# Latent attention scores: the pass of rotated query highs with rotated key lows as 64-row tiles in two halves of TensorE's array

## What is computed

```python
q = jnp.concatenate([q_nope, q_rope], axis=-1)      # 128 plain + 64 rotated dimensions per head
k = jnp.concatenate([k_nope, kr broadcast to all heads], axis=-1)   # the rotated key is shared by the heads
ml = softmax_attention(q, k, v)                     # scale 192 ** -0.5, 512 queries x 768 keys
```

## Time and profile before

| | |
|---|---|
| median of three runs | 2656.37 us (2654.33 to 2659.18) |
| profiled execution, its own time | 2650.61 us |
| its span, first to last instruction | 2648.8 us |
| PE busy | 2523.6 us, 95% |
| DVE / ACT / POOL busy | 60% / 44% / 29% |
| mean granted TensorE clock | 0.980 of full speed |
| share of PE in the chain that ended last | 79% |

### The profile page before, as it was taken

One profiled execution on the slowest core, in us unless ns is written; L12 is line 12 of the kernel. 1 busy time (PEld: TensorE's weight loads), 2 busy tenths in 40 slices (PEclk: granted clock), 3 DMA queues, 4 the chain that ended last, 5 costly groups with the idle time before them and its releaser, 6 DMA issues.

```text
span 2648.8 us, 41477 instructions
## 1 busy us (share of the span) xinstructions
PE 2523.6 (95%) x15654; PEld 2237.8 (84%) x15654; DVE 1587.1 (60%) x2593; ACT 1162.3 (44%) x2137; POOL 773.9 (29%) x462
## 2 busy tenths in 40 slices
PE   7999999999889899899999999999899999899999
PEld 5999999696856787899999978998778868788887
DVE  4877785978677615877866768733776661411111
ACT  4544432555578413323323346634666662322221
POOL 3000012626357332445645520000000013344443
PEclk9999999899889999999999999999999999999999
DMA  7344455021220320332444423424763302122222
GB/s 283 129 143 142 141 173 208 32 73 60 103 96 17 120 80 25 104 112 98 150 135 136 136 80 128 167 92 143 241 205 124 111 32 80 66 98 99 102 97 80
DMA packets 124354, 307.22 MB, mean 116 GB/s; under 512 B 12448, under 2 KB 38048, under 8 KB 122784
## 3 DMA queue, kind: packets, MB, share of 16 engines
q1 hardware_dynamic: 103312, 259.94, 28.9%
q10 hardware_dynamic: 20880, 45.10, 4.9%
HBM read 249.10 MB, written 55.84 MB: 115 GB/s over the span
## 4 chain that ended last, share of the span: by engine, by line
PE 79%; DVE 8%; ACT 6%; issue 5%; POOL 1%; DMA 1%; ACTq 0%; DVEq 0%; SPq 0%; POOLq 0%
PE ps L565 15%; PE ps L567 15%; PE ps L566 15%; PE ps L1603 4%; PE ps L1604 3%; PE ps L1605 3%; PE ps L1498 3%; PE ps L1474 2%; PE ps L1484 2%; PE ps L882 2%; ACT prb L2288 1%; PE ps L1378 1%; PE ps L1380 1%; PE ps L1379 1%; DVE nmd L2809 1%
## 5 line engine op out<-in xcount | busy, mean ns | idle before, releaser
L546 POOL TENSOR_TENSOR Wl<-raws,Wh 128x2048 fp32r<-128x2048 f32 (+3 forms) x82 | 320.4, 3908 | 1495.8 <-ACT Wh L540 1486.8
L565 PE MATMUL ps<-Hh,Wh 128*128 128x384 f32 (+2 forms) x1088 | 375.6, 345 | 8.5 <-DVE xT L3285 2.8
L567 PE MATMUL ps<-Hh,Wl 128*128 128x384 f32 (+2 forms) x1088 | 370.2, 340 | 0.0
L566 PE MATMUL ps<-Hl,Wh 128*128 128x384 f32 (+2 forms) x1088 | 370.1, 340 | 0.0
L540 ACT ACTIVATE Wh<-raws 128x2048 fp32r<-128x2048 f32 (+3 forms) x125 | 204.9, 1640 | 180.4 <-PE ps L567 138.7
L3274 DVE SCALAR_TENSOR_TENSOR xT<-ps,mod,xT 128x384 f32<-128x384 f32 (+3 forms) x174 | 84.5, 533 | 277.1 <-PE ps L567 276.8
L565 PEld LDWEIGHTS ps<-Hh,Wh 128*128 128x128 f32 x1088 | 205.1, 189 | 18.1 <-DVE Hl L2814 5.0
L566 PEld LDWEIGHTS ps<-Hl,Wh 128*128 128x128 f32 x1088 | 205.3, 189 | 6.2 <-issue 1.9
L567 PEld LDWEIGHTS ps<-Hh,Wl 128*128 128x128 f32 x1088 | 205.1, 189 | 4.8
L2939 DVE SCALAR_TENSOR_TENSOR ybuf<-ubuf,vec,ybuf 128x770 f32<-128x770 f32 x144 | 155.5, 1080 | 56.9 <-ACT ybuf L1806 42.4
L565 PE MATMUL ps<-H1h,Wh 128*128 128x512 f32 (+1 forms) x368 | 141.7, 385 | 4.4 <-DVE H1l L2814 3.4
(11 more groups left out here) (494 smaller groups left out, 6725.6 us busy)
## 6 DMA issues: line engine op xcount, KB each, us to landing
raws<-in_slabs SPq DMA_DIRECT2D x218, 512.0 KB, 4.5
adl<-in_ada ACTq DMA_DIRECT2D x48, 512.0 KB, 3.7
ada<-in_ada SPq DMA_DIRECT2D x32, 512.0 KB, 3.8
raws<-in_slabs SPq DMA_DIRECT2D x62, 256.0 KB, 3.4
chunks<-obuf ACTq DMA_DIRECT2D x48, 256.0 KB, 2.1
ada<-in_ada SPq DMA_DIRECT2D x8, 1024.0 KB, 4.9
chunks<-uh SPq DMA_DIRECT2D x17, 384.0 KB, 2.8
lows<-ul SPq DMA_DIRECT2D x17, 384.0 KB, 2.6
```

The source lines that it names most:

```text
L546: nc.gpsimd.tensor_tensor(Wl[n % 2][:, 0:w], raw[n % 2][:, 0:w], Wh[n % 2][:, 0:w].bitcast(f32), ALU.subtract).then_inc(sig("slab_lo"), 1)
L565: nc.tensor.matmul(o, lhs(c)[0], rhs(c, t0, t1)[0], start=(s == 0), stop=False)
L566: nc.tensor.matmul(o, lhs(c)[0], rhs(c, t0, t1)[1], start=False, stop=False)
L567: last = nc.tensor.matmul(o, lhs(c)[1], rhs(c, t0, t1)[0], start=False, stop=(s == k - 1))
```

## The change

The fifth term leaves the loop over the four ranges. Behind it stand four matmuls of 64 rows each, one for each range, in the order 1, 0, 3, 2 of `four`. Block 0 takes the rotated query's high rows from mrs, partitions 0 to 63; block 1 takes them from a new tile mrt, partitions 64 to 127, into which a seventh transfer loads them. Each multiplies by the half of krl that lies in the same partitions. The product low x low, which the fifth term held before, is no longer computed. The matmul of range 0 raises at_beside and the one of range 2 waits for it. As every item now raises at_beside once, the count shared becomes 12 * i + n. ml_in counts 112.

```diff
--- before.py
+++ after.py
@@ -467,6 +467,7 @@
         das, dak, mkh, mkl, mqh, mql, mrs = ([place(f"{n}{j}", at + (b0, b1)[j], shape, f32r) for j in range(2)] for n, at, b0, b1, shape in (
             ("das", 0, 64, 81, [2, LAT]), ("dak", 8, 64, 81, [2, T]), ("mkh", 0, 20, 95, [T]), ("mkl", 0, 0, 98, [T]),
             ("mqh", 0, 12, 101, [LAT]), ("mql", 0, 14, 103, [LAT]), ("mrs", 0, 6, 105, [LAT])))
+        mrt = [place(f"mrt{j}", kb, [LAT], f32r) for j, kb in enumerate((117, 85))]
         krh, krl = place("krh", 28, [T], f32r), place("krl", 68, [T], f32r)
         av, mv = [place("av0", 16, [T]), place("av1", 138, [T])], [place("mv0", 3, [T]), place("mv1", 78, [T])]
         uqh = [place(f"uqh{j}", 148 + 3 * j, [T], f32r) for j in range(2)]
@@ -1443,7 +1444,7 @@
             def scores(i, n):
                 kind, hh, x = ITEMS[n % 12]
                 if x == 0:
-                    name, count = (f"da_in{hh}", 64) if kind == "da" else (f"ml_in{hh}", 96)
+                    name, count = (f"da_in{hh}", 64) if kind == "da" else (f"ml_in{hh}", 112)
                     pe.wait_ge(sig(name), past(name) + count * (i + n // 12) + count)
                     if kind == "ml":
                         pe.wait_ge(sig("kr_in"), past("kr_in") + 64)
@@ -1451,9 +1452,9 @@
                 b0 = 3 * ((n + 1) % 2)
 
                 four = ((1, 0, 256, b0 + 1, 256), (0, 0, 512, b0, 0), (0, 512, T, b0 + 1, 0), (1, 256, T, b0 + 2, 0))
+                shared = 12 * i + n
                 if kind == "da":
                     tq = slice(x * P, (x + 1) * P)
-                    shared = 8 * i + sum(ITEMS[m % 12][0] == "da" for m in range(n))
                     for z, y in BESIDE:
                         b, t0, t1, bank, c = four[z]
                         if (z, y) == (2, 0):
@@ -1469,10 +1470,19 @@
                     tq = slice((2 * x + b) * P, (2 * x + b + 1) * P)
                     qh, ql, qr, kh, kl = (t[hh] for t in (mqh, mql, mrs, mkh, mkl))
                     terms = ((qh[:, tq], kh[:, t0:t1]), (qh[:, tq], kl[:, t0:t1]), (ql[:, tq], kh[:, t0:t1]),
-                             (qr[:, tq], krh[:, t0:t1]), (qr[:, tq], krl[:, t0:t1]))
+                             (qr[:, tq], krh[:, t0:t1]))
                     for y, (q, k) in enumerate(terms):
-                        ins = nc.tensor.matmul(ps[:, bank, c:c + t1 - t0], q, k, start=(y == 0 and (b, t0) != (0, 512)),
-                                               stop=(y == len(terms) - 1), skip_group_check=True)
+                        nc.tensor.matmul(ps[:, bank, c:c + t1 - t0], q, k, start=(y == 0 and (b, t0) != (0, 512)),
+                                         stop=False, skip_group_check=True)
+                for z in (1, 0, 3, 2):
+                    b, t0, t1, bank, c = four[z]
+                    rows, tq = slice(64 * b, 64 * b + 64), slice((2 * x + b) * P, (2 * x + b + 1) * P)
+                    if z == 2:
+                        pe.wait_ge(sig("at_beside"), shared + 1)
+                    ins = nc.tensor.matmul(ps[:, bank, c:c + t1 - t0], (mrs, mrt)[b][hh][rows, tq], krl[rows, t0:t1],
+                                           start=False, stop=True, skip_group_check=True)
+                    if z == 0:
+                        ins.then_inc(sig("at_beside"), 1)
                 ins.then_inc(sig("at_s"), 1)
 
             def turned(i, n, j):
@@ -3929,6 +3939,8 @@
             for half, name in enumerate(("chunks", "lows")):
                 sp.dma_start(mrs[hh][64 * half:64 * half + 64, :].bitcast(f32), scr[name][24 + i, 64 * hh:64 * hh + 64, 0:LAT])\
                     .then_inc(sig(f"ml_in{hh}"), 16)
+            sp.dma_start(mrt[hh][64:P, :].bitcast(f32), scr["chunks"][24 + i, 64 * hh:64 * hh + 64, 0:LAT])\
+                .then_inc(sig(f"ml_in{hh}"), 16)
 
         def heads_ml_queries(sp, i, hh):
```

## The result

| | before | after |
|---|---|---|
| median (22 runs each) | 2656.72 us | 2660.81 us |
| ratio after to before | | 1.0015, 95% interval 1.0009 to 1.0021 |
| span of the profiled execution | 2648.8 us | 2658.8 us |
| PE busy | 2523.6 us | 2532.2 us |

The ratio times 2656.7 is 4.0 us, with 2.4 to 5.6 as its interval. The forecast was +5.1 us, 2661.5 in a range of 2655.5 to 2665. The loss is smaller than the 0.2% that the prediction took as the least that can be told from no change, but with 22 runs on each side the interval does not hold zero: the change costs time.

A forecast was written before the change was run, and what follows sets the result against it. The prediction took PE, busy for 95% of the span, as the bound. Latent items 15 x 0.31 + 0.16 = 4.8 us plus 0.3 for the transfer made 5.1 us, carried to the median 2661.5 us, range 2655.5 to 2665.

The forecast's parts named there:

- Way in: PE going from full-width matmuls to the 64-row tiles in a latent item: the drain costs 0.093 us.
- Wait: Fourth tile's weight load waits for the signalling 256, whose signal comes in order of issue: load at T0 + 0.56 us.
- T0: Start time of the first pair of 64-row tiles in the latent item's new pass.
- Way out: PE's return from tiles to full width: work back at T0 + 0.863 us, first transpose 0.056 us longer.
- the 3.8 that was named as a sign: Expected in the profile after: the latent item's piece of the chain at about 3.8 us instead of 3.51.
- One item: One latent item's new pass takes 1.01 us in place of 0.70: 0.31 us longer.
- Transfer: The added mrt transfer for each head pair, delaying a values store before attention: 0.3 us, bounds 0 and 1.5.
- Sum: Whole kernel: 4.8 us from the latent items plus 0.3 us from the transfer, 5.1 us slower.
- rival B: In the tiled pass, the signal comes with the 256's own end: +3.0 us, 2659.4 us; chance 0.14.
- C: The wait is hidden or the added time disappears in PE's idle time: about +0.3 us, 2656.7 us; chance 0.10.
- D: The latent item's fifth pass is halved by tiling: 5.3 us saved, 2651.1 us; chance 0.05.
- E: The pass's four tiles stream one behind the other: 0.42 us an item, +7.0 us, 2663.4 us; chance 0.19.

The follow-up runs named there:

- swap: The change with the signalling 256 issued ahead of the other half's 512 (order 0, 1, 3, 2): ratio to the kernel before 1.0008 (0.9997 to 1.0019).
- nopass: The kernel before with the fifth term of the latent scores left out: ratio 0.9964 (0.9954 to 0.9975).
- t_only: The kernel before with only the seventh transfer (mrt, read by nobody) and the count 112 added: ratio 1.0000 (0.9991 to 1.0008).
- twice: The change without its wait, both shared-bank ranges in the low half, its four tiles issued twice: ran once, no ratio; period 15.82 us.
- serial: The change with all four tiles in the low half, without wait, mrt or its transfer: ratio to the kernel before 1.0024 (1.0012 to 1.0036).
- nowait: The change with both shared-bank ranges in the low half, so no wait is needed: ratio to the kernel before 1.0006 (0.9997 to 1.0015).
- moved: The kernel before with the fifth term issued at the item's end, still full width, without wait, mrt or transfer: ratio 1.0009 (0.9999 to 1.0019).

## Why the prediction was right

Step by step, forecast and measured:

- *Way in*, 0.093: the first tile at 0.31 where 0.23 would have been, 0.08 to 0.09. Right.
- *Wait*, load at T0 + 0.56: 0.56. And its reason holds: swap moved it to 0.44 (0.45 expected). DVE waits for the latent item 0.17 us longer each time (34.4 against 32.2 us over thirteen items), where 0.16 was forecast.
- *Way out*, back at T0 + 0.863, first transposes 0.056 longer: 0.87, and 0.59 for four transposes on the chain where they had 0.44 behind a full-width matmul, which holds part of the drain too. Right. But the item's own piece of the chain is 3.68 us (2.81 + 0.87), not the 3.8 that was named as a sign: the chain is cut at a matmul's recorded end, so 0.15 of the added time stands in the transposes' piece.
- *One item*, 0.31: period longer by 0.32. Right, and passed on one to one (nopass).
- *Transfer*, 0.3 (0 to 1.5): about 0.5 by the profiles, 0.0 in the single one of t_only; the runs can't tell. The size holds, but the working was partly wrong. The later store that it looked at (its wait grew by 0.63) is covered by the slack of 1.1 us. The earlier store, which it left out because its issue isn't moved, is waited for 0.07 to 1.4 us longer in the five kernels with the transfer than in the kernel before. Why it lands later isn't shown.
- *Sum*, 5.1: measured 4.0, 2.4 to 5.6. By the periods it is 15 x 0.32, and 0.21 for the first item where 0.16 was forecast (13.48 us to the next one in place of 13.27): 5.0, and the transfer on top.

The total alone would not have told the forecast from rival B, whose +3.0 us also lies within 2.4 to 5.6; the trace of the pass does. Rival B (the early signal) falls with the 0.56 and with swap, C with nopass, D with the pass itself, E with twice, since the tiles do run side by side. Tiles that do run one behind the other, without a wait, cost 0.34 an item (serial), close to the change's 0.32. What the prediction could not see, since no run of before had a pass of four tiles alone, was the split of the loss; nowait gives a part of it: at least 0.2 us for the wait and its open load. The other 0.1 it can't share out between the drains, the first pair's loads and its own uneven halves.

What stays open: between the sum by the periods (with the transfer about 5.5) and the ratio's centre lie 1.5 us, just inside its interval. The profiled executions can't settle it, because they differ by whether the granted clock falls near the end of the stage. In the profile of before it is 0.86 from 2150 to 2160 us, in that of the change 1.00, which is no effect of the edit that any run here shows: moved, with the pass full width, has 1.00 there too.

## What to carry to other kernels

Two 64-row tiles side by side shorten the streaming (0.45 us in place of 0.70 in twice), but here a pass of four matmuls is too short to pay for going in and out of the tiled form; count the drain (0.09), the first loads in the open (0.10), the way back (about 0.10, an estimate from the sums above, and 0.06), and only then the saving, 0.25 us for each further pass. A signal from one tile to another should be issued ahead of longer work of the other half, not behind it. And ask of each item of a repeated period by itself whether it lies on the path: here a gain in one kind counted in full and a gain in the other not at all.

## What the runs showed of the hardware

- A matmul's semaphore comes in order of issue, not when its own half is done: with a 512 issued ahead of the 256, the waiting load starts 0.56 us after the pair, with the 256 ahead 0.44. The reordered differential item, 1.25 us in place of 1.35, says the same.
- Starts are not in order of issue across the halves. In nowait the second and fourth tiles (256, low half) form one group from 2005.58 that lasts 0.50; the fourth, which takes 0.28, starts at 2005.80, while the third (512, high half), issued ahead of it, starts at 2005.91. The Trainium skill, TensorE: Matmul & The Clock Gate, section The mechanism, has matmuls in strict order in start and end; the signals agree here, the starts do not. The ends can't decide it, since the profile models them (2006.08 for the fourth tile, 2006.30 for the third).
- The way back to full width costs one open weight load too: the first transpose takes 0.33 us, later ones 0.27.
